# An encoder trunk on one core: the inverse roots of the last key unit move to GpSimd, two dilated scores and a table load move forward

## The reference

```
def rms_norm(x, g):
    xf = x.astype(jnp.float32)
    y = xf * lax.rsqrt(jnp.mean(xf * xf, axis=-1, keepdims=True) + NORM_EPS)
    return (y * g.astype(jnp.float32)).astype(x.dtype)

oa = neighbourhood_attention(rms_norm(split_heads(qa, NA_HEADS), qk_gain[0, 0]),
                             rms_norm(split_heads(ka, NA_HEADS), qk_gain[0, 1]),
                             split_heads(va, NA_HEADS), rpb)
oc = dilated_attention(rms_norm(split_heads(qc, DIL_HEADS), qk_gain[2, 0]),
                       rms_norm(split_heads(kc, DIL_HEADS), qk_gain[2, 1]),
                       split_heads(vc, DIL_HEADS), slopes[SWA_Q_HEADS:])
```

## Time and profile before

| what | value |
|---|---|
| median of 3 runs (lowest to highest) | 2587.18 us (2585.36 to 2587.97) |
| the profiled execution | 2582.92 us, span 2581.2 us |
| busy: PE, DVE, ACT, POOL | 96%, 65%, 41%, 23% of the span |
| first dilated tiles of layer one, layer two | from 273 us, from 1553 us |
| mean granted TensorE clock | 0.988 of full speed |

### The profile page before, as it was taken

The page is one execution under the profiler, slowest core; times in us unless marked ns, Lnnn a source line. Parts: engine busy times, 40 slices in busy tenths (PEclk is TensorE's granted clock), DMA queues, the critical chain, the costliest instruction groups (busy, mean ns, idle before and its releaser), DMA issues.

```text
span 2581.2 us, 36144 instructions
## 1 busy us (share of the span) xinstructions
PE 2477.1 (96%) x12576; PEld 2054.9 (80%) x12576; DVE 1689.7 (65%) x3172; ACT 1061.0 (41%) x2078; POOL 583.2 (23%) x484
## 2 busy tenths in 40 slices
PE   6999899999899999999979998999998999999997
PEld 5987787778688888888778877877877888888886
DVE  4289657863755555689843986678647555556896
ACT  3333556654422222343343336566453222323432
POOL 1000212310445445200000002122115445441000
PEclk9999899999999999999989999999999999999999
DMA  5311430033122221531232115200332222227213
GB/s 182 96 49 41 105 85 14 20 115 110 49 87 85 74 82 49 203 139 55 70 124 89 49 33 127 63 20 20 117 102 74 74 90 82 64 59 275 72 54 115
DMA packets 229542, 220.37 MB, mean 85 GB/s; under 512 B 48880, under 2 KB 190576, under 8 KB 229360
## 3 DMA queue, kind: packets, MB, share of 16 engines
q1 hardware_dynamic: 229360, 218.07, 26.7%
HBM read 169.96 MB, written 48.06 MB: 84 GB/s over the span
## 4 chain that ended last, share of the span: by engine, by line
PE 45%; DVE 3%; ACT 1%; issue 1%; ACTq 0%; DVEq 0%
PE psum L2217 15%; PE psum L1960 4%; PE psum L1962 4%; PE psum L1961 4%; PE psum L2088 3%; PE psum L2250 3%; PE psum L2251 3%; PE psum L2252 3%; PE psum L2066 3%; PE psum L2050 1%; PE psum L2040 1%; DVE T L1415 0%; DVE OPL_t L1694 0%; DVE XN L1301 0%; DVE WL L1688 0%
## 5 line engine op out<-in xcount | busy, mean ns | idle before, releaser
L2217 PE MATMUL psum<-OPH_t,WH 128*128 128x512 f32 x704 | 276.4, 393 | 16.8 <-DVE WL L1688 7.6
L2217 PE MATMUL psum<-OPH_t,WL 128*128 128x512 f32 x704 | 275.4, 391 | 0.0
L2217 PE MATMUL psum<-OPL_t,WH 128*128 128x512 f32 x704 | 275.1, 391 | 0.0
L1688 DVE TENSOR_TENSOR WL<-RAW,WH 128x512 fp32r<-128x512 f32 x132 | 162.0, 1227 | 161.0 <-ACT WH L1170 161.0
L2250 PE MATMUL psum<-ABH 128*128 128x512 f32 x616 | 240.1, 390 | 1.1 <-DVE X L1774 1.1
L2251 PE MATMUL psum<-ABL,ABH 128*128 128x512 f32 x616 | 239.7, 389 | 0.0
L2252 PE MATMUL psum<-ABH,ABL 128*128 128x512 f32 x616 | 239.7, 389 | 0.0
L1034 ACT ACTIVATE T<-T,G 128x192 f32<-128x192 f32 (+3 forms) x352 | 165.9, 472 | 136.7 <-DVE G L1415 134.4
L2217 PE MATMUL psum<-OPH_b,WH 128*128 128x512 f32 x528 | 205.7, 390 | 0.0
L1930 POOL TENSOR_TENSOR WS<-RAW 128x512 f32<-128x512 f32 x88 | 157.4, 1789 | 212.5 <-PE psum L1962 169.5
L2217 PE MATMUL psum<-OPH_b,WL 128*128 128x512 f32 x528 | 205.4, 389 | 0.0
(11 more groups left out here) (219 smaller groups left out, 5376.7 us busy)
## 6 DMA issues: line engine op xcount, KB each, us to landing
RAW<-in_w_gu SPq DMA_DIRECT2D x176, 256.0 KB, 3.8
WDS<-in_w_down SPq DMA_DIRECT2D x88, 256.0 KB, 2.6
UR<-in_w_in SPq DMA_DIRECT2D x56, 256.0 KB, 3.2
g_mid<-GRES SPq DMA_DIRECT2D x28, 512.0 KB, 2.6
WDK<-in_w_down SPq DMA_DIRECT2D x44, 256.0 KB, 6.0
x_res<-X SPq DMA_DIRECT2D x2, 4096.0 KB, 13.7
PR<-in_w_out SPq DMA_DIRECT2D x32, 256.0 KB, 4.9
X<-x_res SPq DMA_DIRECT2D x2, 4096.0 KB, 14.3
```

What stands on the lines that cost most here:

```text
L1688: v.tensor_tensor(WL[SLOT[i, j]][:, :, :], w_source(i, j), WH[SLOT[i, j]][:, :, :].bitcast(F32), ALU.subtract).then_inc(w_lo, 1)
L2217: last = t.matmul(dst[:, :], w[SLOT[i, j]][:, k, :], h[o][:, k, :], start=(i in (1, 5, 6) and k == 0 and part == 0), stop=(i in (2, 3, 4) ...
```

## The change

It has four parts, in both layers. (1) TensorE makes the scores of dilated tiles 0 and 1 before `square_sums` of result 27 instead of after it, and VectorE's minimum of tile 0 comes before the low part of result 27's squares; the minimum of tile 1, which writes over those squares' tile, waits for that low part. (2) ScalarE makes an exponential of one column after the square root of result 25, so that the table is loaded there; for results 26 and 27 it writes the variance plus epsilon (function Identity) instead of the root, the second after the exponential of tile 0. (3) GpSimd raises the variances in RM_LAST to the power -0.5, 128 columns at a time, two pieces after each of its stages for c3 round 0 sections 2 and 3 and round 1 sections 0 and 1. (4) VectorE's reciprocals of RM_LAST are gone; its two scalings go to tile 9 of c3's second round (tile 33 of all) and tile 9 of c2's first (tile 57), each behind a wait for four pieces.

```diff
+            ROOTS_AT = {("c3", 0, 2): 0, ("c3", 0, 3): 2, ("c3", 1, 0): 4, ("c3", 1, 1): 6}
+            SCALE_AT = {("c3", 1, 9): 0, ("c2", 0, 9): 1}
...
+                def qk_variance(i, slot):
+                    act.wait_ge(ss_s, i + 1)
+                    a.activation(RM_LAST[:, slot, :], bank[4 + slot][:, :], ACT.Identity, bias=eps[:, :],
                                  scale=1.0 / HD).then_inc(rmsq_s, 1)
...
-                qk_unit_steps(QT - 1, 1, last=True)
-                qk_rms(2 * QT - 1, 1)
+                qk_square(QT - 1, 0, 1)
+                qk_rms(2 * QT - 3, 1)
+                a.activation(warm[:, :], eps[:, :], ACT.Exp)
+                qk_square(QT - 1, 1, 1)
+                qk_variance(2 * QT - 2, 0)
...
                 exponential(plan[0][0], 0)
+                qk_variance(2 * QT - 1, 1)
                 run(act, act_body)
...
-                def finish_last(s):
-
-                    hf, part = (s - 3) // 6, (s - 3) % 6
-                    if not (s >= 3 and hf < 2 and part < 5):
-                        return
-                    i = 2 * QT - 2 + hf
-                    if part < 4:
-                        r = RM_LAST[:, hf, 128 * part:128 * part + 128]
-                        dve.wait_ge(rmsq_s, i + 1)
-                        v.reciprocal(r, r).then_inc(rec_s, 1)
-                    else:
...
+                square_low(QT - 1, 0)
+                qk_finish(QT - 2, 1, 0)
+
+                def scale_last(hf):
+
+                    dve.wait_ge(root_s, 4 * hf + 4)
+                    to, raw, root = scaled(QT - 1, hf, product_bank(QT - 1, hf, 1), RM_LAST[:, hf, :])
...
                 tmin(plan[0][0], 0, True)
+                square_low(QT - 1, 1)
+                dve.wait_ge(sq_lo, 2 * QT)
                 tmin(plan[0][0], 1, True)
...
+                        if (bd["kind"], bd["i"], q) in ROOTS_AT:
+                            first = ROOTS_AT[bd["kind"], bd["i"], q]
+                            pool.wait_ge(rmsq_s, 2 * QT - 1 + first // 4)
+                            pool.wait_ge(staged, bd["Q"] + 2 * q + 2)
+                            for part in range(first, first + 2):
+                                r = RM_LAST[:, part // 4, P * (part % 4):P * (part % 4) + P]
+                                g.tensor_tensor(r, r, neghalf[:, :].broadcast_to([P, P]), ALU.pow).then_inc(root_s, 1)
+                                pool.wait_ge(root_s, part + 1)
...
-                square_sums(2 * QT - 1, 1)
...
                 score(plan[0][0], 0)
                 score(plan[0][0], 1)
+                square_sums(2 * QT - 1, 1)
                 run(pe, pe_body)
```

More of the change, by code:

```diff
@@ L352, in build_program @@
             b_shift, b_fac, c_shift, c_fac, c_merged = (sem(n) for n in ("b_shift", "b_fac", "c_shift", "c_fac", "c_merged"))
-            merge_s = sem("merge_s")
+            merge_s, root_s = sem("merge_s"), sem("root_s")
             gvar_s, grstd_s, y_s = ([sem(f"{n}_{f}") for f in "abc"] for n in ("gvar_s", "grstd_s", "y_s"))
@@ L419, in product_bank @@
                 return bank[2 * hf + par] if isinstance(u, int) and u >= QT - 2 else bank[2 * par + hf]
-            def rms_of(i, slot):
-                return RM_LAST[:, slot, :] if isinstance(i, int) and i >= 2 * QT - 2 else RM[:, slot, :]
+            ROOTS_AT = {("c3", 0, 2): 0, ("c3", 0, 3): 2, ("c3", 1, 0): 4, ("c3", 1, 1): 6}
+            SCALE_AT = {("c3", 1, 9): 0, ("c2", 0, 9): 1}
             def body(kind, i, T0, U0, G0, Q0):
@@ L999, in qk_rms @@
                         act.wait_ge(qk_s, i - 1)
-                    a.activation(rms_of(i, slot), bank[4 + slot][:, :], ACT.Sqrt, bias=eps[:, :],
+                    a.activation(RM[:, slot, :], bank[4 + slot][:, :], ACT.Sqrt, bias=eps[:, :],
+                                 scale=1.0 / HD).then_inc(rmsq_s, 1)
+                def qk_variance(i, slot):
+                    act.wait_ge(ss_s, i + 1)
+                    a.activation(RM_LAST[:, slot, :], bank[4 + slot][:, :], ACT.Identity, bias=eps[:, :],
                                  scale=1.0 / HD).then_inc(rmsq_s, 1)
@@ L1359, in qk_unit_steps @@
                     square_low(u, 1)
-                    if not last or u < QT - 1:
-                        qk_finish(u, 0, par)
+                    qk_finish(u, 0, par)
                 qk_unit_steps(0, 0, first=True)
@@ L1372, in _ @@
                 qk_unit_steps(QT - 2, 0, last=True)
-                qk_unit_steps(QT - 1, 1, last=True)
-                def finish_last(s):
-                    hf, part = (s - 3) // 6, (s - 3) % 6
-                    if not (s >= 3 and hf < 2 and part < 5):
-                        return
-                    i = 2 * QT - 2 + hf
-                    if part < 4:
-                        r = RM_LAST[:, hf, 128 * part:128 * part + 128]
-                        dve.wait_ge(rmsq_s, i + 1)
-                        v.reciprocal(r, r).then_inc(rec_s, 1)
-                    else:
[L1386 to L1389, removed]
+                square_low(QT - 1, 0)
[3 more added lines that the diff above has]
+                    to, raw, root = scaled(QT - 1, hf, product_bank(QT - 1, hf, 1), RM_LAST[:, hf, :])
+                    v.scalar_tensor_tensor(to, raw, g_qk[:, bass.ds(l * QT + QT - 1, 1)], root,
+                                           op0=ALU.mult, op1=ALU.mult).then_inc(qk_s, 1)
                 def tmin(bd, s, gate):
@@ L1613, in dve_body @@
                         if dilated(bd):
-                            if bd["kind"] == "c3" and b == 0:
-                                finish_last(s)
+                            if (bd["kind"], b, s) in SCALE_AT:
+                                scale_last(SCALE_AT[bd["kind"], b, s])
                             if bd["kind"] == "c2" and b == 1 and s % 6 == 1:
```

## The result

| kernel | median us | runs, lowest to highest | profiled execution |
|---|---|---|---|
| before | 2587.57 | 4, 2585.36 to 2588.66 | 2582.92, span 2581.2 |
| changed | 2883.97 | 4, 2882.49 to 2886.63 | 2883.03, span 2881.3 |

The changed kernel takes 1.1148 times as long (95% interval 1.1129 to 1.1167), 296 us more. The forecast of 2575.0 us has the wrong sign, and 2884 lies far outside the range of 2570 to 2612.

The account below looks back on a forecast made before the run. TensorE, busy 96% of the span, bounds the kernel; gains lie where it waits or clocks low, as at each layer's hand-over. 2 x 2.2 + 6.8 + 4.5 - 2 x 0.8 - 1.9 = 12.2 us less: 2575.0 us, range 2570 to 2612.

Parts of the forecast that it names:

- Roots on GpSimd: GpSimd's powers of 128 columns between stage copies: 1.1 us each, free up to 1.6 us, so no cost.
- rival 2: GpSimd's power takes twice VectorE's reciprocal, 1.9 us; loss 4.8 us, so 7.4 us faster, 2579.8 us; chance 0.10.
- Rival 1: Slow column-by-column roots hold up GpSimd's stage copies and TensorE; at p = 4, 26 us slower, 2613 us; chance 0.34.
- p: Time of one GpSimd power of 128 columns; each microsecond beyond 1.6 us was to cost 8 us a layer.
- head: Hand-over to the dilated heads: scores wait only for result 25, first copy 2.2 us earlier a layer.
- sections, layers one and two: First dilated sections, freed of VectorE's reciprocals and scalings, run undisturbed at 4.40 us: 6.8 and 4.5 us won.
- scalings: VectorE's two scalings, returning at tiles 33 and 57, are partly uncovered by its waits: 0.8 us lost a layer.
- clock at the head: TensorE's first clock fall, after the hand-over, may stay: 0 to 3.9 us lost in all, middle 1.9 us taken.
- table load's cover: ScalarE's early table load fits its idle time before result 27's squares: no cost; otherwise up to 1.4 us a layer.
- SP's queue: SP's 4.6 us turn per group falls back 0.2 us a section, 1.6 us over eight: no cost.
- Rival 4: Only the hand-over's gain counts, as TensorE's low clock holds the sections: 2 x 2.2 us, 2583 us; chance 0.10 shared with another rival.

Follow-up runs that it names:

- kernel without roots: The changed kernel with its eight GpSimd powers a layer turned into multiplications of the same operands, so the result is wrong; median 2568.72 us, ratio 0.9937 to the kernel before.
- The two parts alone: Kernel before with only early scores, early table load and variances, square root omitted: 2575.91 us; kernel before with only last reciprocals and scalings moved to c2: 2578.07 us.
- three-step version: The changed kernel with inverse roots made on VectorE in c2 by three Newton steps instead of GpSimd's powers, computing everything; median 2574.62 us, again 2576.77 us.

## Why the prediction was wrong

**The step that failed** is the price in "Roots on GpSimd": "I read the 548 ns mostly as the length of the computation and its start, with columns following at twice the multiplication's rate", 1.1 us. Measured: 20.72 us. Of the 548 ns about 390 are fixed and 159 are the column, 35 times the 4.6 ns that I let a column have. The one row that I had can't divide itself into start and rate, as the text said; but the choice then fell on the end that suited the change. An unknown with bounds of 0.3 and 70 us, of which more than 1.6 us does harm, is not answered by taking a value near the lower bound with 0.56 of the chance (0.46 and rival 2's 0.10). Rival 2's figure, from the Trainium skill's rule of a factor of two ("GPSIMD Engine Reference", When to use GPSIMD and Key points), would have failed as well: here the factor is 20.72 / 0.94 = 22. The first of these sections speaks of adding, multiplying and taking the larger, the second of elementwise work in general; I carried the factor over to a power, which neither names.

**Rival 1 was the case**, by its mechanism and place: stage copies queued behind the roots, TensorE waiting with a section's first score, four times a layer. Its sum holds with the true p: 8 x (20.72 - 1.6) = 153 us a layer, measured 156 by the stage copies; of the 3 us more, 2 are the section at the low clock after the last wait, and 1 is that stage and two powers take 43.7 us and not 2.0 + 41.4. Its chance of 0.34 was low, and the range ended at p = 4 although the text itself had "over 1000 us" at the upper bound.

**The rest of the sum was near, with one term missing**, as the kernel without roots shows. The terms, for both layers together:

| term | forecast us | measured us |
|---|---|---|
| head | 2 x 2.2 | 2 x 2.5 |
| sections, layers one and two | 6.8 + 4.5 | (26.4 - 19.4) + (24.1 - 19.4) = 6.9 + 4.7 |
| scalings | -2 x 0.8 | -2 x 0.3 |
| clock at the head | -1.9 | 0 |
| stage copy behind GpSimd's, in c2 | not in the sum | -2 x 0.85 |
| table load's cover, SP's queue | 0 | 0 |

Layer one's 19.4 us runs from the first copy, 276.04 us, to the stage copy at 295.49 in the kernel without roots, layer two's from 1546.93 to 1566.36. The measured terms add up to 5.0 + 11.6 - 0.6 - 1.7 = 14.3 us. The profiled executions give 2582.92 - 2568.72 = 14.2, the medians 2584.6 - 2568.7 = 15.9 with an interval from 12 to 20. **The clock** was the term that I couldn't read and put in the middle of its bounds: the fall at 276 us belongs to the idle head, since it stays where only the reciprocals move and goes where only the head does. In the kernel without roots the granted clock is 1.00 from 272 to 310 us. The table load's cover was judged right (ScalarE idle ahead of the squares, now 2.53 us after the load), but it was worth 0.7 us a layer and not the 1.4 us at the load's old place.

**Rival 4** ("only the head counts") falls: moving the reciprocals alone gives 6.5 us, so VectorE, and not only the clock, held those sections. The two parts alone, 8.7 and 6.5 us, add up to 15.2 us, against 15.9 for both together; each of the three is known to 3 or 4 us, so that the sum comes out so near is in part luck.

## What to carry to other kernels

Price an operation at two sizes before it is placed in front of anything that is waited for: from one size, start-up and rate can't be told apart, and an error of 0.16 us a column became 296 us. Where the bounds of a price reach far beyond the slack of what is queued behind it, take the slack as the question, not the best value, and give the far end its chance. And look along the engine that is to be relieved before moving work off it: VectorE had room for the same work a few sections later.

## What the runs showed of the hardware

- **GpSimd's power** to -0.5 on 128 partitions costs 0.39 us and 0.159 us a column, straight from 1 to 128 columns; a multiplication with the same operands takes 0.40 us for 128 columns.
- **VectorE's stage copies aren't slowed beside a power**: from 278 to 285 us, with a power running, they keep 0.57 to 0.59 us. What a step with two operands in SBUF would do there no run shows.
- **VectorE is slowed beside GpSimd's copies**: a step of 0.68 us becomes 0.91 to 1.60, and the copy goes from 1.22 to 1.48. A stage copy of VectorE that starts 0.04 to 0.09 us behind GpSimd's takes 1.17 to 1.22 us instead of 0.61 and ends 0.4 us after it; one that starts 0.19 us ahead of GpSimd's keeps 0.61. That GpSimd and VectorE contend for memory where VectorE's instruction has two operands there, or runs in a mode that takes two ports, is what the Trainium skill says ("GPSIMD Engine Reference", Key points); the steps of the three-step version agree. In which mode the stage copies run, and why a power leaves them alone, no run shows.
- **TensorE's granted clock** was 0.52 while it stood idle for 36 us, and stayed at 0.53 through the whole section of 6.4 us that followed, with TensorE busy for 6.32 of 6.40 us of it. After the third wait it was 0.50 from 408.2 to 411 us and 1.00 from 413 to 414.5.
